# Chunk opening of an RWKV-7 recurrence: the first doubling level released by VectorE's fourth operation, the key scores masked in the last level, the bonus term behind the levels

## What is computed

```python
def _rwkv7_scan(s0, r, w, k, v, a, b):
    def step(S, inp):
        r_t, w_t, k_t, v_t, a_t, b_t = inp
        sa = jnp.einsum('bhvk,bhk->bhv', S, a_t)
        S = S * w_t[:, :, None, :] + sa[..., None] * b_t[:, :, None, :] + v_t[..., None] * k_t[:, :, None, :]
        return S, jnp.einsum('bhvk,bhk->bhv', S, r_t)
...
        bonus_f = jnp.sum(rh * k_dir[:, :, 0] * rw_r_k[0].astype(f32), axis=-1, keepdims=True)
        bonus_b = jnp.sum(rh * k_dir[:, :, 1] * rw_r_k[1].astype(f32), axis=-1, keepdims=True)
        bonus = (bonus_f + bonus_b) * vh
```

## Time and profile before

| | |
|---|---|
| runs, median (lowest to highest) | 3222.06 us (3222.06 to 3226.5), 3 runs |
| profiled execution, own time | 3222.01 us |
| its span, first to last instruction | 3220.1 us |
| mean granted TensorE clock | 0.965 of full speed |
| busy: TensorE / VectorE / ScalarE | 94% / 60% / 44% of the span |
| time of the recurrence in the span | 350 to 482 us (context) and 549 to 680 us (latent) |

### The profile page before, as it was taken

One profiled execution on the slowest core, in us unless ns is written; L12 is line 12 of the kernel. 1 busy time (PEld: TensorE's weight loads), 2 busy tenths in 40 slices (PEclk: granted clock), 3 DMA queues, 4 the chain that ended last, 5 costly groups with the idle time before them and its releaser, 6 DMA issues.

```text
span 3220.1 us, 66623 instructions
## 1 busy us (share of the span) xinstructions
PE 3020.7 (94%) x27360; PEld 2255.0 (70%) x27360; DVE 1941.0 (60%) x3608; ACT 1424.9 (44%) x2294; POOL 8.0 (0%) x17
## 2 busy tenths in 40 slices
PE   5998797989999989889999999999999999999998
PEld 3866694976888876743333333369988999998998
DVE  3768767664333243666666666666685666667566
ACT  3334223223222143556666666654457344445543
POOL 0000000000000000000000000000000000000000
PEclk8998897999999999989999999999999999999999
DMA  5232306012232242259999999955543555543454
GB/s 212 96 129 92 131 4 229 4 34 79 92 98 92 97 146 72 94 219 377 384 378 379 389 378 404 372 206 184 181 131 105 189 182 170 182 157 119 147 180 156
DMA packets 123298, 585.25 MB, mean 182 GB/s; under 512 B 13440, under 2 KB 17024, under 8 KB 88896
## 3 DMA queue, kind: packets, MB, share of 16 engines
q1 hardware_dynamic: 122544, 575.57, 49.3%
q0 software_dynamic: 528, 6.43, 0.5%
HBM read 580.89 MB, written 1.05 MB: 181 GB/s over the span
## 4 chain that ended last, share of the span: by engine, by line
PE 83%; DVE 9%; ACT 3%; DMA 2%; issue 1%; SPq 1%; DVEq 0%; ACTq 0%
PE ps L2408 21%; PE ps L311 16%; PE ps L312 16%; PE ps L313 16%; DMA ada_late<-wada 1%; PE ps L1743 1%; PE ps L1732 1%; PE ps L828 1%; PE ps L1740 1%; DVE w_lo L274 1%; PE ps L2419 1%; PE ps L752 1%; DVE mxv L2122 1%; ACT w_hi L270 0%; DMA w_raw<-wstream 0%
## 5 line engine op out<-in xcount | busy, mean ns | idle before, releaser
L274 DVE TENSOR_TENSOR w_lo<-w_raw,w_hi 128x1024 fp32r<-128x1024 f32 x463 | 565.6, 1224 | 596.4 <-ACT w_hi L270 592.4
L311 PE MATMUL ps<-a_hi,w_hi 128*128 128x256 f32 (+1 forms) x2660 | 838.5, 315 | 47.0 <-DVE a_lo L771 19.1
L312 PE MATMUL ps<-a_lo,w_hi 128*128 128x256 f32 (+1 forms) x2660 | 837.0, 315 | 0.0
L313 PE MATMUL ps<-a_hi,w_lo 128*128 128x256 f32 (+1 forms) x2660 | 833.5, 313 | 0.0
L270 ACT ACTIVATE w_hi<-w_raw 128x1024 fp32r<-128x1024 f32 x463 | 487.5, 1055 | 573.8 <-PE ps L313 526.2
L311 PEld LDWEIGHTS ps<-a_hi,w_hi 128*128 128x128 f32 x2660 | 509.9, 192 | 88.7 <-issue 44.1
L2590 DVE COPY wx<-wset 128x512 f32 x1188 | 424.7, 421 | 224.5 <-PE ps L2408 204.2
L2530 ACT ACTIVATE wx<-wset 128x512 f32 x792 | 444.1, 621 | 217.1 <-PE ps L2408 203.4
L312 PEld LDWEIGHTS ps<-a_lo,w_hi 128*128 128x128 f32 x2660 | 506.3, 190 | 30.8 <-issue 0.5
L313 PEld LDWEIGHTS ps<-a_hi,w_lo 128*128 128x128 f32 x2660 | 505.8, 190 | 31.1
L2408 PE MATMUL ps<-wx,xT 128*32 128x512 f32 x2640 | 378.4, 597 | 5.2 <-DVE wx L2590 5.2
(11 more groups left out here) (522 smaller groups left out, 3736.9 us busy)
## 6 DMA issues: line engine op xcount, KB each, us to landing
wset<-wexp SPq DMA_DIRECT2D x264, 1024.0 KB, 7.8
w_raw<-wstream SPq DMA_DIRECT2D x463, 512.0 KB, 3.3
ada_late<-wada SPq DMA_DIRECT2D x80, 512.0 KB, 6.3
ada_raw<-wada SPq DMA_DIRECT2D x16, 512.0 KB, 9.0
bia<-bias POOLq DMA_DIRECT2D x1, 4096.0 KB, 13.7
con<-consts SPq DMA_DIRECT2D x1, 1824.0 KB, 16.0
conb<-constsb POOLq DMA_DIRECT2D x1, 1224.0 KB, 6.1
hT<-ctxT SPq DMA_DIRECT2D x1, 1024.0 KB, 12.8
```

The costliest lines, as they stand in the source:

```text
L274: nc.vector.tensor_tensor(wlo[:, slot, :], raw[:, slot, :], whi[:, slot, :].bitcast(F32), ALU.subtract).then_inc(lo_ready.sem, 1)
L311: nc.tensor.matmul(out, lhs[0], rhs[0], start=start, stop=False, skip_group_check=skip)
L312: nc.tensor.matmul(out, lhs[0], rhs[1], start=False, stop=False, skip_group_check=skip)
L313: return nc.tensor.matmul(out, lhs[1], rhs[0], start=False, stop=stop, skip_group_check=skip)
```

## The change

`dve_bonus` moves from the head of `dve_solve` to a place behind the five levels. The seven operations of a direction are cut in three. The opening of a direction is now four: `br`, the first level's `nl`, and the two that make `tt[.,0]`, whose last raises `lv_in` itself. After both directions come the two operations for each `tt[.,1]`, the last of which raises `t1_in`; TensorE now waits for `t1_in` in level 0 as well, ahead of T. The masks for `kr` go to the start of the last level, where they raise a new signal `kr_in`, for which TensorE waits ahead of the right sides. Since banks 2 and 3 now hold the key scores until then, the T products go to the upper half of banks 4 and 5. No operation is added or dropped.

```diff
@@ signals
-          "r_ready": ("e2", 16), "r_ps": ("dd", 16)}
+          "r_ready": ("e2", 16), "r_ps": ("dd", 16), "kr_in": ("states", 1)}
@@ pe_solve
                 for d in range(2):
                     pe.wait_ge(*S("x_sb").next("pe"))
-                    if lv > 0:
-                        pe.wait_ge(*S("t1_in").next("pe"))
+                    pe.wait_ge(*S("t1_in").next("pe"))
                     if lv < RLEV - 1:
                         heads_of(d, lambda d, m, e: nc.tensor.matmul(
-                            ps[hp(e), 2 + d, col(m)], tt[hp(e), d, 1, m, :], xs[hp(e), d, m, :],
+                            ps[hp(e), 4 + d, col(m, 1)], tt[hp(e), d, 1, m, :], xs[hp(e), d, m, :],
                             start=True, stop=True)).then_inc(*S("t_ps").one)
...
             for d in range(2):
+                pe.wait_ge(*S("kr_in").next("pe"))
                 heads_of(d, rhs).then_inc(*S("rh_ps").one)
@@ dve_solve
-            dve_bonus(dve, link, seg, n)
+            b4 = lambda i: ps[:, i, :].rearrange("p (m l) -> p m l", m=4)
             for d in range(2):
                 dve.wait_ge(*S("n_ps").next("dve"))
-                b4 = lambda i: ps[:, i, :].rearrange("p (m l) -> p m l", m=4)
                 link(nc.vector.tensor_tensor(br[:, d, :, :], b4(d), bc(mx[:, d, :].unsqueeze(1), [P, 4, P]), ALU.mult))
-
+                link(mask_n(0, d))
                 link(nc.vector.tensor_tensor(tt[:, d, 0, :, :], bank(4 + d),
                                              bc(lvm[:, 0, 0, d, :].unsqueeze(1), [P, 4, RC]), ALU.mult))
-                link(nc.vector.tensor_tensor(tt[:, d, 0, :, :], tt[:, d, 0, :, :], e4, ALU.add))
+                nc.vector.tensor_tensor(tt[:, d, 0, :, :], tt[:, d, 0, :, :], e4, ALU.add).then_inc(*S("lv_in").one)
+            for d in range(2):
                 link(nc.vector.tensor_tensor(tt[:, d, 1, :, :], br[:, d, :, 0:RC],
                                              bc(lvm[:, 1, 0, d, :].unsqueeze(1), [P, 4, RC]), ALU.mult))
-                link(nc.vector.tensor_tensor(tt[:, d, 1, :, :], tt[:, d, 1, :, :], e4, ALU.add))
-                link(nc.vector.tensor_tensor(kr[:, d, :, :], b4(2 + d), bc(mx[:, d, :].unsqueeze(1), [P, 4, P]),
-                                             ALU.mult))
-                link(mask_n(0, d))
-                dve.sem_inc(S("lv_in").sem, 1)
+                nc.vector.tensor_tensor(tt[:, d, 1, :, :], tt[:, d, 1, :, :], e4, ALU.add).then_inc(*S("t1_in").one)
             for lv in range(RLEV):
-                if lv < RLEV - 1:
-                    for d in range(2):
+                for d in range(2):
+                    if lv < RLEV - 1:
                         link(mask_n(lv + 1, d))
+                    else:
+                        nc.vector.tensor_tensor(kr[:, d, :, :], b4(2 + d), bc(mx[:, d, :].unsqueeze(1), [P, 4, P]),
+                                                ALU.mult).then_inc(*S("kr_in").one)
                 for d in range(2):
                     if lv < RLEV - 1:
                         dve.wait_ge(*S("t_ps").next("dve"))
-                        nc.vector.tensor_tensor(tt[:, d, 0, :, :], tt[:, d, 0, :, :], bank(2 + d), ALU.add
+                        nc.vector.tensor_tensor(tt[:, d, 0, :, :], tt[:, d, 0, :, :], bank(4 + d, 1), ALU.add
                                                 ).then_inc(*S("lv_in").one)
...
+            dve_bonus(dve, link, seg, n)
             for d in range(2):
                 dve.wait_ge(*S("yr_ps").next("dve"))
```

## The result

| | before | changed |
|---|---|---|
| median (lowest to highest) | 3222.06 us (3219.31 to 3226.5), 4 runs | 3192.97 us (3191.37 to 3194.32), 4 runs |
| profiled execution, its span | 3222.01, 3220.1 us | 3194.32, 3192.5 us |

The ratio is 0.9911, with a 95% interval of 0.9897 to 0.9926: 29.1 us or 0.9% less. In a second measurement on another occasion it was 3193.91 against 3222.28 us, ratio 0.9919 (0.9906 to 0.9933). The profiled execution of the changed kernel is the slowest of its four; between the two spans lie 27.6 us, and the trace can account for those only.

What follows compares the result with a forecast made beforehand. VectorE was taken to bind the opening from X1 on, TensorE's list elsewhere. Regular openings 16.5, clock 4.2 and eighth chunk 5.8 made 26.5 us off 3222.0: 3195.5 us, range 3191 to 3203 (0.82 or so).

Steps and rivals of the forecast that it cites:

- Where the kernel was bound: Chunk opening: VectorE's seven operations bind from X1 on, TensorE's list before it; 22.1 us idle before X falls under 3.
- The opening of regular chunks: T0 of level 0 starts 2.38 us earlier in five chunks, 2.3 in chunks 1 and 5: 16.5 us.
- The bonus term: Head of regular chunks: moving it saves 0.07 us on VectorE and nothing on the path.
- Level 0 with a late VectorE: Level 0 corrections: VectorE comes 0.3 us late, the lag is gone after two levels; cost 0.
- The last level and the tail: End of each chunk: masks for `kr` and the bonus term fit VectorE's idle time; cost 0.
- The clock: TensorE behind the openings: no drop to half clock once the gap shrinks; 4.2 us for chunks 2, 3 and 6.
- The rival in which the low clock stays: TensorE's clock drops remain despite the shorter gap; 20.8 us gained, 3201 us; chance 0.17.
- The eighth chunk: Opening behind three weight splits, bound by VectorE alone: 5.8 us less, of which 1.2 is the bonus term.
- Outside the recurrence: Preparation between the segments, bound by loads, moves as a whole; loads and clock phase can shift 2 us each way.
- The sum: Whole kernel: 16.5 + 4.2 + 5.8 = 26.5 us off 3222.0, giving 3195.5 us, -0.82%.
- The slower rival: The wait moves to each chunk's tail and the clock falls in all eight: 3230 us; chance 0.02.
- the rival of levels bound by VectorE: VectorE's 0.3 us lag passes to TensorE in each level, some 1 us per chunk: 3205.5 us; chance 0.08.

Runs made afterwards that it cites:

- Experiment 2: Changed kernel with the bonus term moved back to the head of a chunk; 3193.32 us, 0.3 more than the changed kernel.
- experiment 1: Kernel before with only the bonus term moved behind the levels; 3219.42 us against 3221.95, ratio 0.9996.
- Experiment 5: Changed kernel with the key scores' masks back ahead of the levels, behind both releases and the transposed factors; 3201.18 us, ratio to before 0.9937.
- experiment 4: Kernel before with 32 idle-filling identity products on TensorE between X0 and X1's wait, level 0 of each chunk; 3215.84 us against 3222.28, ratio 0.9978.
- the repeat: Changed kernel measured once more, with nothing altered; 3193.91 us against 3222.28 for the kernel before, ratio 0.9919.
- experiment 6: Changed kernel with the key scores' masks back inside each direction's opening, ahead of the release; 3202.68 us, ratio to before 0.9942.

## Why the prediction was right, point by point

- **Where the kernel was bound.** Right: X1 behind the seven operations, TensorE elsewhere. The idle time before X went from 22.1 to 0.9 us (forecast: under 3, in the eighth chunk).
- **The opening of regular chunks**, forecast 16.5 us. Measured 2.3 in the first and fifth and 2.34 to 2.36 in the others, 16.4. Experiment 2 shows it without the bonus term.
- **The bonus term**, forecast 0.07 us on VectorE per chunk and nothing on the path once TensorE bounds the opening. Alone it is 0.14 us a chunk on the path (experiment 1); within the change it is nothing in the regular chunks, as forecast.
- **Level 0 with a late VectorE**, forecast at 0. In the trace the first correction starts at 449.05, 0.80 us behind T0 where it was 0.76, and level 0 takes 3.03 us, 0.05 more. The lag was 0.3 in my working and hardly there on the chip, because I let an unlinked operation hold the next one for 0.43 us, and it is 0.34. Experiment 5 shows how the lag is absorbed when there is one.
- **The last level and the tail**, forecast at 0. Right: no wait of TensorE for `kr` or for the last corrections in any chunk; 3.20 us of idle time are left ahead of the copy, where I said about 2.8. The place in the upper half of banks 4 and 5, bounded by 3 us in all, cost nothing that the levels show: levels 1 to 3 take 3.03 us in both kernels.
- **The clock**, forecast 4.2 us, the least certain term. Right, and the one that experiment 4 settles: the same waits with TensorE kept busy gave back 6.4 us. The rival in which the low clock stays didn't come about. In the changed kernel T (L1739) still stood idle for ScalarE's `xs`, 4.7 us in 30 waits, 0.16 us each, and the clock stayed full in all eight chunks. The Trainium skill's "TensorE: Matmul & The Clock Gate", section "A second HAM failure mode: psum-queue depth-cycling", tells of a kernel whose clock swung between its levels under frequent short idle times. These traces don't show that for idle times of 0.16 us; in the chunks they show the clock lost only behind single gaps of 2.1 us and more.
- **The eighth chunk**, forecast 5.8 us. Measured 5.7 in the profiled pair, where the close match is in part luck, and 6.4 in the repeat (from T0 of chunk 7 to level 1, 40.35 before and 33.91), where its neighbour's 0.7 us stall is not in the stretch. The clock stayed full. The reordering gave a little more than reckoned, mostly by the quicker unlinked operations again: 8.03 us from the end of the splits to level 1's T0, reckoned at 8.71.
- **Outside the recurrence**, forecast unchanged but for 2 us of scatter. The preparation gave 0.7 us between the profiled runs, the stretches ahead of and behind the recurrence 0.2 and 0.3, and these 1.2 us are what the profiled pair saved beyond the sum. The latent chunks start 13.2 us earlier (556.26 to 543.03), forecast 12. My view that the preparation moves as a whole was too plain: for one program it takes 2.4 to 3.4 us more or less from run to run.
- **The sum.** 16.4 + 4.2 + 5.7 + 0.7 + 0.2 + 0.3 = 27.5 of the 27.6 us between the spans, forecast 26.5. The medians differ by 28.4 to 29.1; the further 1 to 1.5 us lie within the scatter of single runs (3190.2 to 3195.6 for the changed kernel) and have no cause that these runs show. A part may lie in the preparation: from level 1's T0 of the fourth chunk to X0 of the fifth it is 90.9 to 92.9 us in the four traces with the old opening (mean 91.9) and 87.9 to 92.5 in the seven with the new one (mean 90.1), but the ranges overlap, and no run tests it.
- **The slower rival**, a wait moved to the tail, and the rival of levels bound by VectorE, are refuted by the same rows; experiments 5 and 6 show how near the second is: 1.28 us more on VectorE ahead of the levels costs 0.57 us a chunk, and 1.20 in the eighth.

## What to carry to other kernels

In a list that an engine works off in order, look for the one item whose wait holds back products that are themselves ready, and count only the operations that this item needs; the rest of its operations can go wherever the timeline shows that engine idle, here ahead of the last level's corrections and ahead of the output's copy. Price a TensorE gap with the clock in mind: a gap of 2.4 us cost itself and, in every second chunk, 1.3 to 1.5 us more in the level behind it, and filling it with useless products was worth 0.2% by itself. A gain of 1.5 us in one stage of a kernel with such scatter is seen in the trace and not in the time.

## What the runs showed of the hardware

- The granted clock of TensorE fell to half behind idle stretches of 2.2 to 2.4 us in about every second chunk (in the eighth 3.2 us; four of eight before, three of eight in experiment 1, and there in other chunks), and behind 2.14 us in the eighth chunk of experiment 6. It didn't fall behind 0.95 us in the eighth chunk of the changed kernel or 1.30 us in that of experiment 2, and where the gap of 2.4 us was filled, no level 0 of sixteen in two runs ran at half clock. The one stretch of it that came in those chunks lay in the eighth chunk of the half-sized fill, from X0 on behind a gap of 2.39 us.
- On VectorE an operation that waits for the end of the one ahead starts 0.46 us after it at 128x256 float32, one that doesn't starts 0.34 us after it, 0.08 us before the other's recorded end: a link costs 0.12 us.
- A 64x64 float32 product is two records of 29 ns each from start to start, so eight of them take 0.47 us.
